# A long fp32 kernel on one core: norm chunks and banks, expert borders, score order, and a gate formed as a row

## The reference, cut to what matters

```python
# first block
h = rmsnorm(x, norm_mix[0]) * (1 + sc1) + sh1
x = x + g1 * gmlp_mixer(h)            # g1 = silu(c) @ ada_w + ada_b: "the gate gm"
h = rmsnorm(x, norm_ffn[0]) * (1 + sc2) + sh2
x = x + g2 * (routed(h) + swiglu(h, shared))      # 64 experts, top 8, width 256
k, v, q = h_kv @ w_k, h_kv @ w_v, h @ w_q          # two modulations of one norm
x = x + g * (attention(q, k, v) @ w_o)             # 16 heads of 64
x = x + g * (routed(h) + swiglu(h, shared))
x = rmsnorm(x, final_norm)
# second block, for l in range(2)
x = x + 0.5 * swiglu_ffn(rmsnorm_2(x, n1[l]))      # width 2816
x = x + hybrid_mixer(rmsnorm_2(x, nm[l]))          # pooling and a linear recurrence
x = x + 0.5 * swiglu_ffn(rmsnorm_2(x, n2[l]))
# then rmsnorm_2(x, final_norm_2)
```

## Time and profile before

| | |
|---|---|
| runs | 3117.77, 3121.77, 3122.19 us; median 3121.77 |
| profiled execution, own time | 3120.01 us, its span 3118.5 us |
| TensorE granted clock, mean | 0.983 |
| TensorE (PE) busy | 3005.1 us, 96% |
| VectorE (DVE) / ScalarE (ACT) / GpSimd (POOL) busy | 1567.3 (50%) / 1071.9 (34%) / 225.1 us (7%) |
| DMA | 770.43 MB, mean 247 GB/s |

### The profile page before, as it was taken

How to read it: one execution, slowest core, us unless ns; L and a number is a source line. 1 busy time by engine, 2 the same in 40 slices (tenths; PEclk the granted TensorE clock), 3 DMA queues, 4 the chain that set the end, 5 groups by cost and what they waited for, 6 DMA issues and landing times.

```text
span 3118.5 us, 42571 instructions
## 1 busy us (share of the span) xinstructions
PE 3005.1 (96%) x17368; PEld 2076.8 (67%) x17368; DVE 1567.3 (50%) x2559; ACT 1071.9 (34%) x1516; POOL 225.1 (7%) x262
## 2 busy tenths in 40 slices
PE   6999999999999989999999998999999999999998
PEld 5985444444444965444444444999879989898898
DVE  6764334444443674232324324557875554579654
ACT  3432222222222562222222224334643343455433
POOL 0300111111110001111111110000000000000000
PEclk9989999999999999999999999999999999999999
DMA  9836789999995536878879785554455555445453
GB/s 341 243 136 256 269 324 365 364 378 368 366 387 219 169 127 255 316 295 328 316 294 373 301 315 200 197 182 158 158 167 189 187 182 186 156 160 195 163 189 108
DMA packets 274331, 770.43 MB, mean 247 GB/s; under 512 B 36928, under 2 KB 186576, under 8 KB 210928
## 3 DMA queue, kind: packets, MB, share of 16 engines
q1 hardware_dynamic: 236016, 715.17, 62.1%
q0 software_dynamic: 29232, 45.43, 4.3%
q10 hardware_dynamic: 8912, 7.40, 0.7%
HBM read 924.08 MB, written 1.05 MB: 297 GB/s over the span
## 4 chain that ended last, share of the span: by engine, by line
PE 90%; DVE 5%; ACT 3%; issue 1%; DMA 1%; DVEq 0%; ACTq 0%; SPq 0%
PE G L1425 22%; PE U L1445 6%; PE B L1445 5%; PE G L1211 5%; PE G L1212 5%; PE U L1211 5%; PE G L1213 5%; PE U L1212 5%; PE U L1213 5%; PE Y L1211 4%; PE Y L1212 4%; PE Y L1213 4%; PE Y L1456 2%; PE Y L1455 2%; PE M L1405 2%; PE U L1405 1%
## 5 line engine op out<-in xcount | busy, mean ns | idle before, releaser
L1804 DVE TENSOR_TENSOR part_lo<-ring,part_hi 128x2048 fp32r<-128x2048 f32 x240 | 548.0, 2288 | 380.9 <-ACT part_hi L869 379.0
L1425 PE MATMUL G<-wide,gathered 128*64 128x512 f32 x2368 | 680.9, 595 | 1.4 <-DMA arena<-in_moe_w_up_dram 1.4
L869 ACT ACTIVATE part_hi<-ring 128x2048 fp32r<-128x2048 f32 x240 | 459.5, 1915 | 469.9 <-PE Y L1213 282.0
L1425 PEld LDWEIGHTS G<-wide,gathered 128*64 128x64 f32 x2368 | 207.4, 137 | 259.2 <-issue 259.2
L1425 PE MATMUL G<-arena,gathered 128*64 128x512 f32 x704 | 312.4, 596 | 0.0
L1211 PE MATMUL G<-h_hi,part_hi 128*128 128x256 f32 x1024 | 296.0, 289 | 10.3 <-DVE h_lo L1862 10.3
L1212 PE MATMUL G<-h_lo,part_hi 128*128 128x256 f32 x1024 | 294.7, 288 | 0.0
L1213 PE MATMUL G<-h_hi,part_lo 128*128 128x256 f32 x1024 | 294.4, 287 | 0.0
L1211 PE MATMUL U<-h_hi,part_hi 128*128 128x256 f32 x1024 | 289.8, 283 | 0.4 <-ACT arena L1161 0.3
L1212 PE MATMUL U<-h_lo,part_hi 128*128 128x256 f32 x1024 | 289.4, 283 | 0.0
L1213 PE MATMUL U<-h_hi,part_lo 128*128 128x256 f32 x1024 | 289.4, 283 | 0.0
(11 more groups left out here) (485 smaller groups left out, 5355.9 us busy)
## 6 DMA issues: line engine op xcount, KB each, us to landing
ring<-in_ffn_w_up_dram SPq DMA_DIRECT2D x88, 1024.0 KB, 5.3
arena<-in_moe_w_down_dram SPq DMA_DIRECT2D x86, 1024.0 KB
wide<-in_moe_w_gate_dram SPq DMA_DIRECT2D x84, 1024.0 KB
wide<-in_moe_w_up_dram SPq DMA_DIRECT2D x84, 1024.0 KB
arena<-in_moe_w_gate_dram SPq DMA_DIRECT2D x44, 1024.0 KB
arena<-in_moe_w_up_dram SPq DMA_DIRECT2D x44, 1024.0 KB
ring<-in_ffn_w_down_dram SPq DMA_DIRECT2D x44, 1024.0 KB, 4.8
wide<-in_moe_w_down_dram SPq DMA_DIRECT2D x42, 1024.0 KB
```

What stands on the lines that cost most here:

```text
L869: eng.activation(part_hi[:, n % SPLIT, :], ring[:, slot, :], ACT.Copy).then_inc(hi_ready, 1)
L1425: last = mm(bank["G"][rows], lhsT=gathered[p // 2 % 2][:, k, at:at + SLOTS], rhs=units[tile][:, :, k, :], start=(k == 0), stop=(k == K - 1 ...
L1804: eng.tensor_tensor(part_lo[:, n % SPLIT, :], ring[:, slot, :], part_hi[:, n % SPLIT, :].bitcast(F32), ALU.subtract).then_inc(lo_ready, 1)
```

## The change

**Gate as a row.** `ada_gm`, its modulation and its spreading go. `row_fill("gm")` multiplies ones by the summed share itself; the bias arrives as a row by one broadcast DMA on GpSimd's queue and is added in the copy out of the bank. **Norms.** `SCALED_BY` says for each tile of each norm who scales it, VectorE (D) or ScalarE (A), or both by halves (DA). Norms 5 to 10 put their chunks in B, M and the first 512 columns of Y. `first_up` multiplies the first unit k by k, alternating between G and U, one column half in each; the second unit goes to B; `silu` of the first goes by halves. `root_table` moves ahead, into the stage before. **Expert borders.** ScalarE evicts G and U and makes the roundings; VectorE evicts B and M and subtracts. The router writes Y and starts after G and B. The first slot table moves behind the first three k-blocks of `up`, which waits for one gathered bank at a time. The shared expert's split goes by halves. **Queries.** Unit 0 goes to Y, k by k in both column halves, and each remainder directly follows its cast. **Attention.** Scores of pair 2 follow unit 9, those of pair 3 unit 10; one conversion (`next_lo`) moves from the loop over pairs to behind it.

```diff
-FILLS = {"ada_first": (0, 2), "ada_gm": (2, 3), "ada_ffn": (3, 5)}
-GAINED = ["gm", "at"]
+FILLS = {"ada_first": (0, 2), "ada_ffn": (3, 5)}
+GAINED = ["at"]
...
+SCALED_BY = {0: ("D", "D"), 2: ("D", "A"), 5: ("D", "DA"), **{n: ("A", "DA") for n in (1, 3, 6, 7, 8, 9, 10)}}
...
+def qkv_bank(f):
+    return ("Y", 0) if f == 0 else (pair_bank(f), f // 2 - (f % 2 == 0))
...
+        def turned_chunk(n, k):
+            if n not in GAINED_NORMS:
+                return bank["GUBM"[k // 2]][:, k % 2, :]
+            if k % 4 < 2:
+                return bank["BM"[k % 4]][:, k // 4, :]
+            at = HALF * (k % 4 - 2) + S * (k // 4)
+            return Y[:, 0, at:at + S]
+        first_query = Y[:, 0, :].rearrange("p (a n) -> p a n", a=2)[:, :, 0:S]
...
+            eng.wait_ge(gv_ready, 1)
+            eng.dma_start(gm_bias, A["ada_b"][0, 2 * D:3 * D].partition_broadcast(P)).then_inc(gm_bias_in, 16)
...
+                def scale(t, cs):
+                    eng.wait_ge(root_over, TT * n + t + 1)
+                    eng.activation(scaled[:, t, cs], x[:, t, cs], ACT.Identity, scale=rms[:, t:t + 1]).then_inc(scaled_act, 1)
+                by = SCALED_BY.get(n, ("", ""))
...
+                    if i == 3 and by[0] == "A":
+                        scale(0, slice(0, D))
...
+                if "A" in by[1]:
+                    scale(1, slice(HALF, D) if "D" in by[1] else slice(0, D))
...
-                    bk = "GUBM"[k % 4]
                     if k < 4:
-                        wait_full(eng, bk, "norm_" + NORMS[n])
+                        eng.wait_ge(bank_turned, 4 * i + k + 1)
                     else:
-                        eng.wait_ge(lo_early, 4 * GAINED_NORMS.index(n) + k - 3)
-                    eng.activation(h_hi[:, k, :], bank[bk][:, k // 4, :], ACT.Identity, scale=gain[:, k:k + 1]).then_inc(out_round, 1)
+                        eng.wait_ge(lo_early, 6 * i + k - 3)
+                    eng.activation(h_hi[:, k, :], turned_chunk(n, k), ACT.Identity, scale=gain[:, k:k + 1]).then_inc(out_round, 1)
...
-                eng.wait_ge(drained["U"], turn * GROUPS_PER_TURN + (b.at["U", key] + n))
-                eng.activation(silu, bank["G"][:], ACT.Silu).then_inc(drained["G"], 1)
+                if n == 1:
+                    wait_drained(eng, "B", "up0_" + key)
+                elif n:
+                    eng.wait_ge(drained["U"], turn * GROUPS_PER_TURN + (b.at["U", key] + n))
+                if n == 0:
+                    for c, bk in enumerate("GU"):
+                        eng.activation(silu[:, c, :], bank[bk][:, 0, :], ACT.Silu).then_inc(drained[bk], 1)
+                else:
+                    eng.activation(silu, bank["G"][:], ACT.Silu).then_inc(drained["G"], 1)
+                if n == FF_UNITS - 1:
+                    root_table()
...
-                norm_out(1 + 2 * m, [(h_out, coef[:, 1 + 2 * m], vec(3 + 6 * m))], 2 + 3 * m)
+                eng.wait_ge(coef_ready, 2 + 3 * m)
+                for q, bk in enumerate("GU"):
+                    wait_full(eng, bk, "norm_" + NORMS[1 + 2 * m])
+                    for c in range(2):
+                        k = 2 * q + c
+                        o = eng.activation(h_out[:, k, :], bank[bk][:, c, :], ACT.Identity, scale=coef[:, 1 + 2 * m, k:k + 1],
+                                           bias=vec(3 + 6 * m)[:, k:k + 1])
+                    o.then_inc(drained[bk], 1)
+                for q, bk in enumerate("GUBM"):
+                    wait_drained(eng, bk, "norm_" + NORMS[1 + 2 * m])
+                    part = slice(2 * q, 2 * q + 2)
+                    eng.activation(h_hi[:, part, :], h_out[:, part, :], ACT.Copy).then_inc(h_round, 1)
...
+            def first_up(parts, stride2, norm):
+                u = [view_a(p) for p in parts]
+                at = 6 * GAINED_NORMS.index(NORMS.index(norm))
+                for k in range(K):
+                    if k in (4, 5):
+                        wait_drained(eng, "BM"[k - 4], "norm_" + norm)
+                    else:
+                        eng.wait_ge(lo_early, at + (k + 1 if k < 4 else k - 1))
+                    for c, bk in enumerate("GU"):
+                        cs = slice(c, None, 2) if stride2 else slice(c * P, (c + 1) * P)
+                        last = exact(bank[bk][:, 0, :], [v[:, k, cs] for v in u], (h_hi[:, k, :], h_lo[:, k, :]),
+                                     k == 0, k == K - 1)
...
+                    if "D" in SCALED_BY[n][t]:
+                        eng.wait_ge(scaled_ready, scaled_count(n, t, "D"))
+                    if "A" in SCALED_BY[n][t]:
+                        eng.wait_ge(scaled_act, scaled_count(n, t, "A"))
+                    for q in range(4):
+                        bk = ("BM", "GUBM")[n not in GAINED_NORMS][q:q + 1]
+                        if t == 0 and bk:
                             wait_free(eng, bk, "norm_" + NORMS[n])
                         for c in range(2):
                             k = 4 * c + q if n in GAINED_NORMS else 2 * q + c
-                            last = eng.transpose(bank[bk][:, c, t * P:(t + 1) * P], scaled[:, t, k::K], ident[:])
+                            last = eng.transpose(turned_chunk(n, k)[:, t * P:(t + 1) * P], scaled[:, t, k::K], ident[:])
                         if t == 1:
-                            last.then_inc(filled[bk], 1)
+                            last.then_inc(bank_turned if n in GAINED_NORMS else filled[bk], 1)
...
+                def up_first():
+                    for bk in "GU":
+                        wait_free(eng, bk, key)
+                    first_up(wait_unit(unit0), True, ready)
+                    wait_free(eng, "B", "up0_" + key)
+                    up_matmuls(wait_unit(unit0 + 1), "B", True)
...
+                        if p == 0:
+                            wait_drained(eng, "UGBM"[k // 2], f"{key}g0_{k // 2}")
...
                 blocks_before()
                 for f, bk in enumerate("UGBM"):
                     gather(0, f, bk)
-                slot_tables(0)
                 for p in range(NP):
                     nb, f = p // 2 + 1, 2 * (p % 2)
                     if p == 0:
                         up(p, (0, 1, 2))
+                        slot_tables(0)
                         turn_tables()
...
-                if n == 18:
-                    ada_fill("ada_gm")
                 if n == 20:
-                    row_fill("gm", gm_diag)
+                    row_fill("gm", share(VECTORS.index(2)))
...
-                wait_free(eng, "M", key + "halves")
-                for bk in "GUB":
-                    wait_drained(eng, bk, "norm_" + NORMS[1 + 2 * m])
+                wait_free(eng, "Y", key + "halves")
                 for k in range(K // 2):
+                    if k % 2 == 0:
+                        for bk in ("GB", "UM")[k // 2]:
+                            wait_drained(eng, bk, "norm_" + NORMS[1 + 2 * m])
                     for half in range(2):
                         rows = slice(half * E, (half + 1) * E)
-                        last = mm(bank["M"][rows, 0, :], lhsT=router[:, m, half * K // 2 + k, :],
+                        last = mm(Y[rows, 0, 0:S], lhsT=router[:, m, half * K // 2 + k, :],
                                   rhs=h_out[:, half * K // 2 + k, :], start=(k == 0), stop=(k == K // 2 - 1), skip_group_check=True)
-                last.then_inc(filled["M"], 1)
+                last.then_inc(filled["Y"], 1)
...
+                def first_queries(parts):
+                    u = [view_a(v) for v in parts]
+                    for k in range(K):
+                        eng.wait_ge(h_ready, 4 * 2 + k // 2 + 1)
+                        for c in range(2):
+                            last = exact(first_query[:, c, :], [v[:, k, c * P:(c + 1) * P] for v in u],
+                                         (q_hi[:, k, :], q_lo[:, k, :]), k == 0, k == K - 1)
+                    last.then_inc(unit_done, 1)
...
+                    if f in (7, 9, 10):
+                        for part in (0, 4) if f == 7 else (1, 5):
+                            bk, before_f = qkv_bank(part)
+                            wait_drained(eng, bk, "qkv", before_f)
+                        for pair in {7: (0, 1), 9: (2,), 10: (3,)}[f]:
+                            scores(pair)
...
-                    if pair + 2 < PAIRS:
+                    if 4 <= pair + 2 < PAIRS:
...
-                    if q:
-                        lo_h(src, q - 1, halves, hi, lo)
-                lo_h(src, 3, halves, hi, lo)
+                    lo_h(src, q, halves, hi, lo)
...
-                    if n in TURNED:
-                        eng.tensor_scalar(scaled[:, t, :], x[:, t, :], rms[:, t:t + 1], None, ALU.mult).then_inc(scaled_ready, 1)
+                    by = SCALED_BY[n][t] if n in SCALED_BY else ""
+                    if "D" in by or n not in SCALED_BY:
+                        eng.wait_ge(root_over, TT * n + t + 1)
+                    if "D" in by:
```

(52 more changed lines are left out.)

138 lines of the change are left out of this document (85 added, 53 removed).

## The result

The changed kernel takes **3082.80 us** (median of 4 runs, 3081.82 to 3083.47) against 3121.83 us (4 runs) before, a ratio of 0.9878 (95% interval 0.9861 to 0.9895). The profiled executions are 3081.82 and 3120.01 us, with spans of 3080.2 and 3118.5 us: 38.3 us less.

A forecast was written before the change was run, and what follows sets the result against it. TensorE, busy 3005.1 of 3118.5 us, was taken as the bound, with idle time, needless instructions and half clock to win; terms summed to 38.5 us off 3120.0, giving 3081.5, or 3083 as a median, range 3073 to 3098.

The forecast's parts named there:

- Gate row: First stage's gate in the down loop: dropping 16 one-column matmuls and half clock behind them saves 6.5 us, bounds 3.1 and 6.5.
- Borders: Norms 6 to 10: first unit starts 5.0 us after E, the last down matmul's end; 2.0 us each, 10.0 in all.
- Norm 5 and queries: Norm 5's longest wait shrinks, saving 1.4 us; query unit 0 no longer waits for bank G, saving 1.7 us.
- Clock: Six second-block norms: of 10.6 us lost at half clock behind restarts, 7.5 us come back.
- Entries to the expert layers: Norms 1 and 3: router starts 2.0 and 2.4 us earlier, h_lo keeps its end; 5.2 us with some clock, bounds 3.0 and 6.5.
- Slot table: Expert layers: first slot table behind three blocks of the up product, both its waits go, 2.4 us.
- shared split: Shared expert's hidden rows split by halves: saves 0.4 us, the second half becoming 0.4 us later.
- Attention: Scores of the third and fourth pairs among value units, conversion moved behind the third output split: 3.4 us, bounds 1.2 and 5.
- 1: Rival: the clock falls at every border all the same, so 7.5 + 1.5 us are lacking: 3092 us; chance 0.18.
- 2: Rival: VectorE becomes the bound, 1 us short at six borders and attention's gain halved, 8 us lacking: 3091 us; chance 0.09.
- 3: Rival: norm relay not sped up, ScalarE's 1024-column scaling costs over 2 us, eight borders lose 1.1 us: 3092 us; chance 0.06.
- 4: Rival: alternating banks breaks matmul overlap in seven units, 0.289 us each instead of 0.12, +57 us: about 3140 us; chance 0.04.

## Why the prediction came out as it did

- **Gate row**: right, 6.6 us for 6.5, and for the reason given. The lower bound of 3.1 would have needed a clock that falls anyway; the clock is 1.00 at that place without the products, which excludes that.
- **Borders**: E + 5.16 for E + 5.0. The bank step is right: from the transposes to the unit 1.64 us for 1.68. The relay gave 0.17 us instead of 0.34 (1.13 us for a scaling estimated at 1.06, its second half 0.72 instead of 0.63). I called this gain little "because the work went to the engine that holds the chain", and the run with VectorE's scaling puts a number on it: 0.55 us a border, the other way.
- **Norm 5 and queries**: 1.5 for 1.4 and 1.7 for 1.7.
- **Clock**: 8.1 us for 7.5. Before, all six restarts fell in both profiles (10.6 and 10.9 us). After, the loss is 3.5 in the mean of eleven, so the term is worth 7.2. "I take most of it back" was the right size, but the argument for it does not hold, so the size was in part luck. It rested on the last border, whose window of rows 6 is at 1.00 up to the restart. These are the windows behind that restart, in the kernel before:

```profile
2920.77:2921.60 0.83, 0.83 (x7) 0.83 (x8) 0.83 (x3) 0.83 (x3) 0.00 (x0) 1.00 0.00 0
2921.60:2925.00 3.40, 3.40 (x19) 3.40 (x18) 3.40 (x3) 2.62 (x2) 0.00 (x0) 0.50 0.00 0
```

  That border did not hold the clock: it fell 0.8 us into the unit and cost 1.5 us, one of the six losses that I had added up myself. That chance picks the borders I had not said either. By my own sign (0.50 for over 3 us behind a border) I was wrong on the clock at norm 7, which has it for 4.4 us. The rule of the Trainium skill ("TensorE: Matmul & The Clock Gate", section "Part 4: PE-mode transpose") that transposes don't count as work would have had the clock fall at every border. The windows above show three borders and their restarts at 1.00 with the same 16 transposes in them, so here it does not decide; no run shows what a transpose counts for.
- **Entries to the expert layers**: 3.9 us for 5.2. At norm 1 the router starts 1.8 us earlier for 2.0 (it waits 0.83 us, and 1.03 at norm 3, for some 0.6), and some 0.8 us of clock came back behind it, counted in the next row of the table. At norm 3 the router starts 2.4 us earlier as forecast, though only because the clock stayed at 1.00 in this profile's border: in nine of the eleven it starts 1.7 to 1.9 us earlier. It also costs 1.49 us less by its clock, yet the first unit comes only 2.1 us earlier. The step that failed is "h_lo keeps its end": at norm 3 a conversion stands between VectorE's evictions and h_lo, as these rows show, and I had costed the roundings alone. It stood there before too, but filled the time in which VectorE waited for ScalarE's evictions. h_lo ends at E + 11.8 where it had ended at E + 10.5.

```profile
1137.38 0.99 DVE L2359 TENSOR_SCALAR arena<-M,coef,ada 128x256 f32<-128x256 f32 x2
1138.28 2.28 DVE L1926 TENSOR_TENSOR part_lo<-ring,part_hi 128x2048 fp32r<-128x2048 f32 x1
1140.48 2.49 DVE L2367 TENSOR_TENSOR h_lo<-arena,h_hi 128x512 fp32r<-128x512 f32 x4
```

- **Slot table**: wrong in its step. 2.4 us forecast, 0.4 measured (15.43 to 15.23 us and 15.63 to 15.44). "TensorE has 12 matmuls more in between" is true of the picks, whose use comes later; but the turned tables need bank M, which VectorE's two reads of the slot table hold, and the block that used to cover these reads now stands ahead of the table:

```profile
255.03 0.44 PE L1509 MATMUL M<-ident,diag 128*128 128x128 f32 x2
256.48 0.60 PE L1476 MATMUL M<-ident,arena 128*64 128x128 f32 x4 [1.01 <-DVE rows_lo L2097]
```

  The shared split is worth 0.6 us for 0.4: the stop is 0.67 us shorter in each layer, but the second half, which I had 0.4 us late, is waited for. The rest of the row is clock, 0.8 us in the first layer's first unit and 1.6 in its shared down product, which no term had and no run explains. So the misses cancel, and the sum came out closer than its terms.
- **Attention**: 4.4 us for 3.4. Of that, 0.9 us is clock in the first query unit, which was in no term: 5.5 us at half before, 3.4 after. The rest, 3.5, has the term's size: 1.5 us behind the moved conversion for 1.2, and 2.0 from the scores for 2.2. But of these 2.0 about 0.8 is the clock behind the third pair's stop, and the order alone gave 1.2.
- **Rivals**: 1 needed the clock to fall at every border as before, which it does when the unit is held, and did in one of the eleven profiles with short borders. 2 did not come: no first or second unit behind norms 5 to 10 waits for a conversion (at norm 3 one is in the way, as told above). 3 is true in kind (the scaling does hold the chain) and far too large in size, 1.13 us and not over 2. 4 is excluded by the pitch of 0.121 us.

## What to carry to other kernels

When a wait is removed by moving an instruction, look at what its result holds (here a bank), not only at who uses the result: the block that was moved ahead had been the cover of the next wait. Work that a relay hands to a less busy engine is lost if that engine holds the chain; take away what stood in that engine's way first (the table load) and then ask again who should do the rest. When a product starts on the first half of its operand, follow it to the matmul that needs the second: half of what the shorter stop gave was lost there. Count the idle time ahead of a restart twice, once as idle and once for the clock behind it: holding the first unit by 1.9 us a border cost 12 us of idle time and 6 of clock.

## What the runs showed that was not expected

The clock behind a border is steady for the long borders (two profiles of the kernel before fall behind the same norms, with losses of 10.6 and 10.9 us) and a matter of the moment for the short ones (1 to 5 of the five later borders in eleven profiles, 2, 3 and 3 of them in the three of one and the same kernel). Eight one-column products of 3.7 us went with half clock for 6.8 us in one place and 13.7 in another, where a row fill follows them. Both put steps of 1.5 us and more into single executions, so that edits of 3 us, plain in the stretches of a profile, don't show in medians of four runs.
